# State space scan of a hybrid mixer: step sizes in the projection's last half, turns in another order, VectorE's and ScalarE's rounds reordered

## The reference

```python
# a stream's features
xbc = jax.nn.silu(_grid_dwconv(xbc, conv_w, grid_hw) + conv_b)
xs, bm, cm = jnp.split(xbc, [SSD_INNER, SSD_INNER + SSD_GROUPS * SSD_N], axis=-1)
dt_f = jax.nn.softplus(dt_f_raw + dt_bias_f)    # step sizes, 8 heads; dt_b alike
a_f = dt_f * -jnp.exp(a_log_f)
# one step of _ssd_scan on a chunk
cum = jnp.cumsum(ac.astype(jnp.float32), axis=1)
seg = cum[:, :, None] - cum[:, None, :]
lmat = jnp.exp(jnp.where(mask[None, :, :, None], seg, -jnp.inf))
scores = jnp.einsum("bihn,bjhn,bijh->bhij", cc, bc, lmat)
intra = jnp.einsum("bhij,bjhp->bihp", scores, xc * dtc[..., None])
inter = jnp.einsum("bihn,bhpn->bihp", cc, s) * jnp.exp(cum)[..., None]
w = (jnp.exp(tot[:, None] - cum) * dtc)[..., None]
s_new = s * jnp.exp(tot)[:, :, None, None] + jnp.einsum("blhn,blhp->bhpn", bc * w, xc)
# _merge_heads
y = (y_ssd + d_skip[:, None] * f["xs"]).reshape(b, t, SSD_INNER) * jax.nn.silu(f["z"])
o_ssd = rms_norm(y.reshape(b, t, SSD_GROUPS, -1), ssd_norm.reshape(SSD_GROUPS, -1))
```

## Time and profile before

| | |
|---|---|
| runs | 3858.15, 3865.59, 3862.91 us; median 3862.91 |
| profiled execution, its own time | 3863.12 us |
| its span, first to last instruction | 3860.9 us |
| mean granted TensorE clock | 0.919 |
| busy: PE, DVE, ACT, POOL | 3421.4, 1987.5, 1422.2, 212.5 us |
| setup of the SSD | 424.7 to 446.0 us of the span |
| states and gates | 446.0 to 498.0 us |
| rounds | 498.0 to 684.0 us |

### The profile page before, as it was taken

One profiled execution on the slowest core, in us unless ns is written; L12 is line 12 of the kernel. 1 busy time (PEld: TensorE's weight loads), 2 busy tenths in 40 slices (PEclk: granted clock), 3 DMA queues, 4 the chain that ended last, 5 costly groups with the idle time before them and its releaser, 6 DMA issues.

```text
span 3860.9 us, 51017 instructions
## 1 busy us (share of the span) xinstructions
PE 3421.4 (89%) x20390; PEld 2841.1 (74%) x20390; DVE 1987.5 (51%) x2849; ACT 1422.2 (37%) x2116; POOL 212.5 (6%) x225
## 2 busy tenths in 40 slices
PE   1998755574999999999898999999999989999998
PEld 1776533462777877788865769999999556699998
DVE  6648466835644444435554454355444544444433
ACT  2532444213433233324334444233333344433322
POOL 1000022210000000000010000000000200000000
PEclk9999876556999999999998989999999989899999
DMA  5562000003323322423210002342332000023333
GB/s 195 180 204 87 29 17 20 25 6 137 126 93 115 115 93 93 159 92 102 94 39 28 15 9 70 92 158 83 118 131 65 25 28 23 2 95 103 117 92 104
DMA packets 94652, 326.01 MB, mean 84 GB/s; under 512 B 10384, under 2 KB 11664, under 8 KB 93520
## 3 DMA queue, kind: packets, MB, share of 16 engines
q1 hardware_dynamic: 75168, 247.56, 19.8%
q0 software_dynamic: 18528, 74.07, 5.4%
q10 hardware_dynamic: 720, 1.12, 0.1%
HBM read 297.48 MB, written 25.30 MB: 84 GB/s over the span
## 4 chain that ended last, share of the span: by engine, by line
PE 76%; DVE 13%; ACT 5%; issue 4%; DMA 2%; DVEq 0%; POOL 0%; ACTq 0%; SPq 0%; POOLq 0%
PE psum L146 72%; DVE mixer L167 4%; PE psum L149 3%; DVE mixer L177 2%; DVE wlo L167 1%; DVE arena L167 1%; DVE junk L181 1%; DVE arena L190 1%; ACT arena L155 1%; ACT whi L159 1%; ACT arena L154 1%; DVE mixer L194 1%; ACT region L159 1%; DVE region L167 1%; ACT arena L159 0%
## 5 line engine op out<-in xcount | busy, mean ns | idle before, releaser
L146 PE MATMUL psum<-region,whi 128*128 128x260 f32 (+2 forms) x9152 | 1993.8, 315 | 58.1 <-ACT whi L159 31.2
L146 PEld LDWEIGHTS psum<-region,whi 128*128 128x128 f32 (+1 forms) x9152 | 1493.7, 188 | 182.8 <-issue 61.0
L146 PE MATMUL psum<-region,wlo 128*128 128x260 f32 (+2 forms) x4576 | 1432.2, 313 | 0.0
L167 DVE TENSOR_TENSOR wlo<-stage,whi 128x1024 fp32r<-128x1024 f32 (+2 forms) x454 | 512.9, 1130 | 774.3 <-ACT whi L159 742.5
L146 PEld LDWEIGHTS psum<-region,wlo 128*128 128x128 f32 (+1 forms) x4576 | 864.3, 189 | 55.3
L159 ACT CAST whi<-stage 128x1024 fp32r<-128x1024 f32 (+2 forms) x454 | 441.6, 973 | 257.9 <-PE psum L146 175.0
L146 PE MATMUL psum<-arena 128*128 128x65 f32 (+8 forms) x2064 | 424.4, 357 | 8.7 <-ACT arena L155 7.8
L146 PE MATMUL psum<-mixer 64*128 64x128 f32 (+6 forms) x1172 | 251.3, 463 | 158.1 <-DVE mixer L167 147.9
L146 PEld LDWEIGHTS psum<-mixer 64*128 64x128 f32 (+2 forms) x1172 | 179.0, 293 | 230.8 <-issue 111.6
L159 ACT COPY arena<-psum 128x512 f32<-128x512 f32 (+10 forms) x428 | 190.3, 445 | 429.7 <-PE psum L146 396.3
L146 PEld LDWEIGHTS psum<-arena 128*128 128x128 f32 (+4 forms) x2064 | 255.9, 181 | 107.6 <-issue 92.3
(11 more groups left out here) (130 smaller groups left out, 2502.3 us busy)
## 6 DMA issues: line engine op xcount, KB each, us to landing
stage<-in_w SPq DMA_DIRECT2D x144, 512.0 KB, 3.5
stage<-in_wi SPq DMA_DIRECT2D x55, 512.0 KB, 4.2
stage<-in_wm SPq DMA_DIRECT2D x48, 512.0 KB, 3.3
stage<-in_wo SPq DMA_DIRECT2D x48, 512.0 KB, 3.5
stage<-in_wg SPq DMA_DIRECT2D x44, 512.0 KB, 3.3
stage<-in_wu SPq DMA_DIRECT2D x44, 512.0 KB, 3.3
stage<-in_wd SPq DMA_DIRECT2D x32, 512.0 KB, 3.3
arena<-xr_scratch POOLq DMA_DIRECT2D x7, 2080.0 KB, 9.6
```

The costliest lines, as they stand in the source:

```text
L146: return Issued(self, self.e and self.e.matmul(out, w, x, start=start, stop=stop, skip_group_check=True))
L167: return Issued(self, e and e.tensor_tensor(out, a, b, op))
```

## The change

First, what depends on the step sizes alone moves from the setup into the last half of the projection: ten transposes of 128x16, the softplus, `dA`, the sums and their six exponentials, `wsf` and `et2` (`pe_steps`, `act_steps`, `dve_steps`). Second, the tiles are turned in the order `TURNS`, four before the states and six between them; B's ten turns go into three banks, copied by three instructions; the first gate batch follows state step 6, and `SUMMED` moves. Third, in the rounds: ACT runs `act_states` first, then dt1 and Eb, and then two squares that leave their sums, followed by the square root; DVE's reduce is gone, and its y sums stand at the end of the round. PE's and POOL's order in the rounds is not edited. Helper lines behind L156 are four higher after the change.

```diff
+    def square_sum(self, out, a, total):
+        e = self.own()
+        return Issued(self, e and e.activation(out, a, ACT.Square, bias=0.0, scale=1.0, accum_out=total))
...
+    def pe_steps(e, kk):
+        T, A, D = sssd.pe, sssd.act, sssd.dve
...
+            for t in range(10):
+                ins = e.transpose(psum[:, b, t * 16:t * 16 + 16], ld[32:48, t * 128:(t + 1) * 128],
+                                  C["ident"][32:48, 32:48])
+            ins.then_inc(*T.up("dt"))
...
+        if kk == 2:
+            b, free = bank.take("cums", A, "eto")
...
+    def act_steps(e, kk):
+        T, A, D = sssd.pe, sssd.act, sssd.dve
+        w0 = dx.rearrange("p (a b) -> p a b", b=16)
+        if kk == 0:
+            e.wait_ge(*D["dt0"])
+            e.activation(w0, dtk, ACT.Abs).then_inc(*A.up())
+            e.activation(w0, w0, ACT.Exp, scale=-1.0).then_inc(*A.up())
+            e.activation(al, R["alog"], ACT.Exp).then_inc(*A.up())
+            e.activation(w0, w0, ACT.Ln, bias=ONEC).then_inc(*A.up("sp"))
+        if kk == 2:
+            e.wait_ge(*T["cums"])
+            v = psum[:, bank.of["cums"], :].rearrange("p (a b) -> p a b", b=8)
+            for d in range(2):
+                s8 = slice(d * 8, d * 8 + 8)
+                e.activation(ecf[:, :, s8], v[:, d * 10:d * 10 + 10, :], ACT.Exp).then_inc(*A.up())
+                e.activation(wsf[:, :, s8], v[:, 20 + d * 10:30 + d * 10, :], ACT.Exp).then_inc(*A.up())
+                e.activation(eto[:, :, s8], v[:, 40 + d * 10:50 + d * 10, :], ACT.Exp).then_inc(*A.up())
+            A.mark("eto")
...
+    def dve_steps(e, kk):
...
+        if kk == 0:
+            for m in (4, 5):
+                e.wait_ge(*sproj.act["conv", m])
+            e.wait_ge(*T["dt"])
+            e.tensor_tensor(dtk, psum[:, bank.of["dt"], 0:160].rearrange("p (a b) -> p a b", b=16),
+                            R["dtb"][:, None, :].broadcast_to([128, 10, 16]), ALU.add).then_inc(*D.up("dt0"))
+        if kk == 1:
+            e.wait_ge(*A["sp"])
+            e.scalar_tensor_tensor(dtk, dtk, 0.0, w0, ALU.max, ALU.add).then_inc(*D.up())
+            e.scalar_tensor_tensor(dA, dtk, -1.0, al[:, None, :].broadcast_to([128, 10, 16]), ALU.mult,
+                                   ALU.mult).then_inc(*D.up("dA"))
+        if kk == 3:
+            e.wait_ge(*A["eto"])
+            e.tensor_tensor(wsf, wsf, dtk, ALU.mult).then_inc(*D.up())
+            for d in range(2):
+                e.tensor_copy(et2[0:64, :, d, :], eto[0:64, :, d * 8:d * 8 + 4]).then_inc(*D.up())
+                e.tensor_copy(et2[64:128, :, d, :], eto[64:128, :, d * 8 + 4:d * 8 + 8]).then_inc(*D.up())
+            D.mark("w")
...
-    SUMMED = {6: 0, 12: 1, 18: 2}
+    SUMMED = {10: 0, 14: 1, 18: 2}
+
+    TURNS = (0, 1, 2, 9, 3, 8, 4, 7, 5, 6)
...
         e.wait_ge(*sproj.act["end"])
-        for t in range(10):
+
+        def turn(t):
             b, free = bank.take(("xt", t), A, "xt", t, among=LOW)
             for f in free:
                 e.wait_ge(*f)
             for m in range(4):
                 ins = e.transpose(psum[:, b, m * 128:(m + 1) * 128], xsrc(m, t), C["ident"])
             ins.then_inc(*T.up("xt", t))
-            b, free = bank.take(("bt", t), D, "bt", t, among=LOW)
+        turn(TURNS[0])
+        turn(TURNS[1])
+        for t0, t1 in BATCH:
+            b, free = bank.take(("bt", t0), D, "bt", t0, among=HIGH)
             for f in free:
                 e.wait_ge(*f)
-            e.transpose(psum[:, b, 0:128], xsrc(4, t), C["ident"])
-            e.transpose(psum[:, b, 128:192], ld[:, t * 128:(t + 1) * 128], C["ident"][0:64, 0:64]).then_inc(
-                *T.up("bt", t))
-        pe_gates(e, 0)
-        b, free = bank.take("cums", A, "eto", among=LOW)
-        for f in free:
-            e.wait_ge(*f)
-        e.wait_ge(*D["dA"])
-        for d in range(2):
-            a_ = dA[:, :, d * 8:d * 8 + 8]
-            e.matmul(psum[:, b, d * 80:d * 80 + 80], C["le" if d == 0 else "ge"], a_, True, True)
-            e.matmul(psum[:, b, 160 + d * 80:240 + d * 80], C["gt" if d == 0 else "lt"], a_, True, True)
-            ins = e.matmul(psum[:, b, 320 + d * 80:400 + d * 80], C["ones"], a_, True, True)
-        ins.then_inc(*T.up("cums"))
+            for t in range(t0, t1):
+                ins = e.transpose(psum[:, b, (t - t0) * 128:(t - t0 + 1) * 128], xsrc(4, t), C["ident"])
+            ins.then_inc(*T.up("bt", t0))
+        turn(TURNS[2])
+        turn(TURNS[3])
...
+                if n < 6:
+                    turn(TURNS[4 + n])
+                continue
+            if r == 6:
+                pe_gates(e, 0)
+            if r in SUMMED:
                 pe_sums(e, SUMMED[r])
...
         sproj.all_end(e)
-        for t in range(10):
+        for t in TURNS:
             e.wait_ge(*T["xt", t])
             e.copy(xtk[:, t, :], psum[:, bank.of["xt", t], :]).then_inc(*A.up("xt", t))
...
-            e.activation(eto[:, :, s8], v[:, 40 + d * 10:50 + d * 10, :], ACT.Exp).then_inc(*A.up())
-        A.mark("eto")
...
         for r in range(12):
+            act_states(e, r - 1)
             j = r
             if j < 8:
                 t = j + 2
...
                 A.mark("dt1", j)
-            act_states(e, r - 1)
-            j = r - 2
-            if 0 <= j < 8:
-                s3 = j % 3
-                e.wait_ge(*D["z", j])
-                e.activation(yb[:, 0, :], ys[:, s3, :], ACT.Square).then_inc(*A.up("sq", j))
-                e.wait_ge(*D["sm", j])
-                e.activation(sm[:, s3, 2:4], sm[:, s3, 0:2], ACT.Sqrt, scale=1.0 / 256, bias=EPSC).then_inc(
-                    *A.up("rt", j))
-            j = r
-            if j < 8:
                 e.wait_ge(*T["D", j, 1])
                 if j >= 3:
                     e.wait_ge(*T["y", j - 3])
                 b = bank.of["D", j]
                 e.activation(Eb[:, j % 3], psum[:, b:b + 2, :].rearrange("p a (b c) -> p (a b) c", c=128),
                              ACT.Exp).then_inc(*A.up("Eb", j))
+            j = r - 2
+            if 0 <= j < 8:
+                s3 = j % 3
+                e.wait_ge(*D["z", j])
+                for g in range(2):
+                    gs = slice(g * 256, g * 256 + 256)
+                    e.square_sum(yb[:, 0, gs], ys[:, s3, gs], sm[:, s3, g:g + 1]).then_inc(*A.up())
+                A.mark("sq", j)
+                e.activation(sm[:, s3, 2:4], sm[:, s3, 0:2], ACT.Sqrt, scale=1.0 / 256, bias=EPSC).then_inc(
+                    *A.up("rt", j))
...
-        for t in range(10):
-            b = bank.of["bt", t]
-            e.wait_ge(*T["bt", t])
-            e.tensor_copy(btk[:, t, :], psum[:, b, 0:128]).then_inc(*D.up())
-            e.tensor_copy(dtk[:, t, :], psum[:, b, 160:176]).then_inc(*D.up("bt", t))
-        d2 = dtk[:, :, :]
...
-        stored_rz(e)
+        for t0, t1 in BATCH:
+            e.wait_ge(*T["bt", t0])
+            e.tensor_copy(btk[:, t0:t1, :], psum[:, bank.of["bt", t0], 0:(t1 - t0) * 128].rearrange(
+                "p (t x) -> p t x", x=128)).then_inc(*D.up("bt", t0))
...
+                e.wait_ge(*A["xt", t])
...
+            if r == 10:
+                stored_rz(e)
...
-                b, b2 = bank.of["y", j], bank.of["in", j]
+                b2 = bank.of["in", j]
                 y0 = ys[:, s3, :]
                 e.wait_ge(*T["in", j])
                 if j >= 3:
                     e.wait_ge(*T["T", j - 3])
+                if j:
+                    e.wait_ge(*A["sq", j - 1])
...
                 D.mark("in", j)
-                e.wait_ge(*T["y", j])
-                e.tensor_tensor(y0, y0, psum[:, b, :], ALU.add).then_inc(*D.up("yi", j))
-                e.tensor_tensor(y0, y0, yb[:, 0, :], ALU.add).then_inc(*D.up())
-                e.wait_ge(*G["yb1", j])
-                e.tensor_tensor(y0, y0, yb[:, 1, :], ALU.add).then_inc(*D.up("y3", j))
-                e.wait_ge(*zd[s3][j])
-                e.tensor_tensor(y0, y0, zt[:, s3, :], ALU.mult).then_inc(*D.up("z", j))
-                e.wait_ge(*A["sq", j])
-                e.tensor_reduce(sm[:, s3, 0:2], yb[:, 0, :].rearrange("p (g x) -> p g x", x=256), ALU.add).then_inc(
-                    *D.up("sm", j))
             j = r - 3
...
             dve_states(e, r - 1, cur_g)
+            j = r - 2
+            if 0 <= j < 8:
+                b, s3 = bank.of["y", j], j % 3
+                y0 = ys[:, s3, :]
+                e.wait_ge(*T["y", j])
+                e.tensor_tensor(y0, y0, psum[:, b, :], ALU.add).then_inc(*D.up("yi", j))
+                e.tensor_tensor(y0, y0, yb[:, 0, :], ALU.add).then_inc(*D.up())
+                e.wait_ge(*G["yb1", j])
+                e.tensor_tensor(y0, y0, yb[:, 1, :], ALU.add).then_inc(*D.up("y3", j))
+                e.wait_ge(*zd[s3][j])
+                e.tensor_tensor(y0, y0, zt[:, s3, :], ALU.mult).then_inc(*D.up("z", j))
         D.mark("end")
```

(25 more changed lines are left out.)

31 lines of the change are left out of this document (4 added, 27 removed).

## The result

The changed kernel takes 3878.28 us (median of six runs, 3872.67 to 3881.66) against 3860.53 for the kernel before in the same comparison (3856.48 to 3866.42): a ratio of 1.0044, with a 95% interval of 1.0031 to 1.0057. It is slower by 17.7 us; 3886 had been predicted, 23.5 more than before. The profiled execution has a span of 3875.1 us against 3860.9.

The account below looks back on a forecast made before the run. No engine is full; a chain across engines sets the pace. Setup and states -3, rounds +19.2, POOL's product +3.3, head -3, tail +7 sum to +23.5 us on 3863.1: 3886, range 3870 to 3899.

Parts of the forecast that it names:

- After, they are in series.: In the rounds: kdt copy, dt1, POOL's sum and yb1, third y sum, rf and E1 follow one another, 2.3 us more per beat.
- The beat of 25.55: One round from PE block start to the next: 25.55 us against 23.24 before; six beats +19.2 us.
- POOL's first product, 1.66 in rounds 2 and 3: First half of dtm on POOL meets DVE's y sums and rf in rounds 2 and 3: 2 x 1.66 = +3.3 us.
- Setup and states, -3: Before the rounds, up to rf(0): setup and states together 3 us shorter, bounds -8 and +4.
- The setup's 14.7 reach the rounds whole: Rival: first state weighting comes 14.7 us earlier and all of it reaches the rounds, giving 3874; chance 0.13.
- Head, -3: From rf(0) to in(0): POOL starts later, part of its overlap with rf goes, -3 us, between -6 and 0.
- Tail, +7: From in(6) to the GLA's first product: late y sums and ACT's late output copy, +7 us, between +4 and +9.
- rival 2: Setup: its 14.7 us reach the rounds whole if ACT's gate chain has slack; 3874, chance 0.13.
- rival 3: Rounds: POOL's first product meets rf in the other four beats too, +6.6 us, 3893; chance 0.11.
- rival 4: Rounds: PE's blocks are granted the full clock, 5.7 us a block, 40 for seven; 3846, faster; chance 0.04.
- were that all: Rounds: DVE's eight reduces and their waits go, 28.0 + 5.5 us; by that alone the beat would shorten.
- The rival of DVE going by PE's products: Rounds: yb1 is not the limit, DVE goes by PE, 21.6 to 23.3 us a beat; 3865 at 22.5; chance 0.08.

## Why the prediction was right

**"After, they are in series."** Right, and shown three ways: cutting the chain at ACT gave 31 us back, cutting it at POOL 18 (most of the other 12 goes with the collision of POOL's late sum with DVE, above), and lengthening dt1 by 3.44 lengthened the beats by 3.9, which it doesn't where dt1 stands early.

**The beat of 25.55.** The three beats with rf and without POOL's other product measured 25.59, 24.75 and 26.03, mean 25.46; the last 22.3 (22.97 predicted). POOL's sum with dt1 started 16.3 behind the block at 566.14 (16.2 predicted).

**POOL's first product, 1.66 in rounds 2 and 3.** The four products of DVE took 5.65 there against 4.15 later: 1.50 each. The first two beats were 26.33 and 26.89, the others as above. The rounds together are 20.4 longer, 22.5 had been summed. Of the 2.1, 0.3 are this term, 0.7 the last beat, 0.7 the first beat, which was shorter than a beat of 25.55 and a collision of 1.50 make, and the rest the other four.

**Setup and states, -3.** Measured -4.8 in the profiled pair (rf behind the totals at 493.2 against 498.1), by errors that partly cancel, so the nearness of this term is in part luck. The first turned tile came at 431.32, 6.6 later, not 3: the exponentials of the sums waited for PE's sums and held ACT in front of the silu copies. And Abs stood at 445.64, 0.9 later than before, where 2.3 earlier had been predicted. The timeline of ACT in the kernel after:

```profile
422.85 1.59 ACT L154 ACTIVATE mixer<-psum 128x80 f32<-128x80 f32 x6 [4.47 <-PE psum L146]
424.53 1.28 ACT L154 ACT_TABLE_LOAD   x1
425.83 1.31 ACT L154 ACTIVATE mixer<-psum 128x512 f32<-128x512 f32 x2
...
431.32 1.26 ACT L163 COPY mixer<-psum 128x512 f32<-128x512 f32 x2 [0.80 <-PE psum L149]
```

But PE's own delay is the larger part. In the kernel with the exponentials later ACT stands idle ahead of the first silu copy of z and waits for PE, and that copy still starts 4.2 later than before. The timelines of ACT before, and in the kernel with the exponentials later:

```profile
418.66 0.60 ACT L154 ACTIVATE mixer<-psum 128x512 f32<-128x512 f32 x1 [7.42 <-PE psum L146]
```

```profile
422.87 0.60 ACT L154 ACTIVATE mixer<-psum 128x512 f32<-128x512 f32 x1 [4.39 <-PE psum L146]
```

Ahead of it PE stands 1.92 before the ten transposes of the step sizes, which take 0.80, and the twelve matmuls of the sums take 1.46 (from 419.93 to 421.39): together those 4.2. The projection's last half also got four table loads (413.40, 415.30, 417.10 and 424.53 in the kernel after), not the two that the prediction counts; only the last stands between the exponentials and the silu copies.

What made up for the late Abs is the chain behind it, which I had taken at its old length: 45.5 in place of 51.2 (to the totals' copies at 491.10). ACT waits 17.2 for PE there, 22.3 before. "The setup's 14.7 reach the rounds whole" was wrong, as forecast: the first weighting came at 434.42, 11.6 earlier, and 4.8 were left at rf(0).

**Head, -3.** -4.3: 19.7 in place of 24.0. The reason given, ACT's order in the rounds, can account for 1.8 of it at most: with the new setup and the old rounds the head was 21.5 already. What the new setup shortens there stays open. **Tail, +7.** +7.9: 38.4 in place of 30.5. The split of it between y sums and ACT's output copy was not right: with the y sums early and the output copy where it was, behind the squares, the tail was 26.5 and 28.2, so it is DVE's late y sums that made it.

**The sum.** At the GLA's first product (703.18 against 684.05) the kernel after is 19.1 behind; 23.5 had been summed, and the difference of 4.4 is that of the terms above: 1.8 in the setup, 1.3 in the head and 2.1 in the rounds, less 0.9 in the tail. The timeline shows the lead of before at 19.9 at the last load of `in_wk` (2956.41 and 2976.35) and at 14.6 at that of `in_mu` (3774.06 and 3788.64), in code that the change doesn't touch, in one pair of executions. The medians differ by 17.7. What gave 5 us in that stretch stays open; over 280 us of it (3100 to 3380 before, 3119.9 to 3399.9 after) the granted clock was 0.89 before and 0.90 after, so the clock can be part of it.

**The rivals.** The setup's lead did not reach the rounds (rival 2), POOL's first product did not meet rf in the later beats (rival 3; it started at 591.97, behind the block's start at 591.73), and the blocks of PE kept the low level of the clock (rival 4).

**What the prediction missed.** It costed the reorder of DVE by its beat alone and called the squares' removal a gain that "were that all" would come. It did not say that the late y sums are a cost of their own wherever dt1 is early: 24.6 us. The rival of DVE going by PE's products at 21.6 to 23.3 a beat was the right picture for that kernel (21.4 in the mean of its four middle beats) and stood in the prediction only as a way in which the forecast could fail.

## What to carry to other kernels

When an instruction of one engine is moved ahead of another in its queue, ask what it waits for, and follow not only the moved work but what is now queued behind that wait on this engine and on the next ones: here eight copies of 3.44 us together, on an engine with idle time to spare, carried two products of GpSimd and two of VectorE into the loop. Two reorderings in one change have to be costed in all their combinations, since one place was the better under one order of ScalarE and the worse under the other. And a slower result can hold good parts: of this change the squares' sums (29 us) and the setup (8 us) were worth keeping, and the two moves beside them, act_states ahead of dt1 and the y sums at the end of the round, hid both.
